# Sample states' old outputs in one padded tile, and side work of the projection in fewer groups

## The reference, cut to what matters

```python
inter = einsum('bthk,bhkv->bthv', qc * exp(b), state)         # outputs of the old states
att   = einsum('bthk,bshk,btshk->bhts', qc, kc, exp(diff))    # inside the chunk
new_state = state * exp(b_last)[..., None] + einsum('bshk,bshv->bhkv', kc * exp(b_last[:, None] - b), vc)
```

## Time and profile before

| what | value |
|---|---|
| median of the runs | 1394.96 us (1394.67 to 1395.44, 3 runs) |
| the profiled execution's own time | 1395.06 us |
| its span, first to last instruction | 1393.4 us |
| granted TensorE clock | 1.000 of full speed |
| PE busy | 1388.3 us (100% of the span) |
| DVE busy | 857.0 us (62%) |
| ACT busy | 583.3 us (42%) |
| POOL busy | 130.7 us (9%) |

### The profile page before, as it was taken

The page is one execution under the profiler, slowest core; times in us unless marked ns, Lnnn a source line. Parts: engine busy times, 40 slices in busy tenths (PEclk is TensorE's granted clock), DMA queues, the critical chain, the costliest instruction groups (busy, mean ns, idle before and its releaser), DMA issues.

```text
span 1393.4 us, 28677 instructions
## 1 busy us (share of the span) xinstructions
PE 1388.3 (100%) x10755; PEld 1375.1 (99%) x10755; DVE 857.0 (62%) x1178; ACT 583.3 (42%) x707; POOL 130.7 (9%) x214
## 2 busy tenths in 40 slices
PE   9999999999999999999999999999999999999999
PEld 9999999999999999999999999999999999999999
DVE  7778877657876555555554445555555556667554
ACT  7556744665334333333333333333333333335332
POOL 1523105001221000000000000000000001111000
PEclk9999999999999999999999999999999999999999
DMA  8756435446554545545445556545454545556553
GB/s 298 204 186 233 142 130 174 143 141 227 181 170 162 166 165 165 166 156 173 159 144 163 163 162 196 168 157 170 156 170 161 165 131 163 164 161 197 184 158 117
DMA packets 76905, 236.60 MB, mean 170 GB/s; under 512 B 14136, under 2 KB 14672, under 8 KB 76472
## 3 DMA queue, kind: packets, MB, share of 16 engines
q1 hardware_dynamic: 72072, 223.43, 50.2%
q0 software_dynamic: 3744, 11.22, 2.7%
q10 hardware_dynamic: 1040, 1.28, 0.3%
HBM read 231.34 MB, written 4.47 MB: 169 GB/s over the span
## 4 chain that ended last, share of the span: by engine, by line
PE 98%; ACT 1%; DVE 1%; DMA 0%; issue 0%; SPq 0%; DVEq 0%; ACTq 0%
PE acc L516 31%; PE acc L518 30%; PE acc L517 30%; PE px L1551 0%; PE px L1669 0%; PE px L1511 0%; PE px L1514 0%; PE px L1517 0%; DMA w_raw<-in_w_in 0%; PE px L1609 0%; PE px L516 0%; PE px L518 0%; PE px L517 0%; PE px L1736 0%; ACT w_hi L462 0%
## 5 line engine op out<-in xcount | busy, mean ns | idle before, releaser
L468 DVE TENSOR_TENSOR w_lo<-w_raw,w_hi 128x1024 fp32r<-128x1024 f32 (+3 forms) x446 | 509.8, 1148 | 313.9 <-ACT w_hi L462 305.0
L462 ACT ACTIVATE w_hi<-w_raw 128x1024 fp32r<-128x1024 f32 (+3 forms) x446 | 439.5, 988 | 551.2 <-PE acc L518 544.3
L516 PE MATMUL acc<-n_hi,w_hi 128*128 128x288 f32 x1664 | 492.5, 296 | 0.0
L517 PE MATMUL acc<-n_lo,w_hi 128*128 128x288 f32 x1664 | 490.9, 295 | 0.0
L518 PE MATMUL acc<-n_hi,w_lo 128*128 128x288 f32 x1664 | 489.2, 294 | 0.0
L518 PEld LDWEIGHTS acc<-n_hi,w_lo 128*128 128x128 f32 x1664 | 313.5, 188 | 0.0
L517 PEld LDWEIGHTS acc<-n_lo,w_hi 128*128 128x128 f32 x1664 | 312.4, 188 | 0.0
L516 PEld LDWEIGHTS acc<-n_hi,w_hi 128*128 128x128 f32 x1664 | 311.8, 187 | 0.0
L516 PE MATMUL acc<-x_hi,w_hi 128*128 128x288 f32 x816 | 244.9, 300 | 0.0
L517 PE MATMUL acc<-x_lo,w_hi 128*128 128x288 f32 x816 | 240.8, 295 | 0.0
L518 PE MATMUL acc<-x_hi,w_lo 128*128 128x288 f32 x816 | 240.0, 294 | 0.0
(11 more groups left out here) (304 smaller groups left out, 889.9 us busy)
## 6 DMA issues: line engine op xcount, KB each, us to landing
w_raw<-in_w_gu SPq DMA_DIRECT2D x176, 512.0 KB, 3.9
w_raw<-in_w_in SPq DMA_DIRECT2D x76, 512.0 KB, 4.3
w_raw<-in_w_down SPq DMA_DIRECT2D x64, 384.0 KB, 3.1
w_raw<-in_w_down SPq DMA_DIRECT2D x64, 320.0 KB, 3.1
w_raw<-in_w_ple SPq DMA_DIRECT2D x32, 576.0 KB, 3.7
w_raw<-in_w_out SPq DMA_DIRECT2D x32, 512.0 KB, 4.2
w_raw<-in_w_in SPq DMA_DIRECT2D x12, 256.0 KB, 6.2
proj<-in_xT SPq DMA_DIRECT2D x8, 288.0 KB, 6.6
```

The costliest lines, as they stand in the source:

```text
L462: nc.scalar.activation(whi[:, slot, 0:kt * P], raw[:, slot, 0:kt * P], ACT.Copy).then_inc(S("w_hi_done"), 1)
L468: nc.vector.tensor_tensor(wlo[:, slot, 0:kt * P], raw[:, slot, 0:kt * P], whi[:, slot, 0:kt * P].bitcast(F32), ALU.subtract).then_inc(S("w ...
L516: nc.tensor.matmul(out, w_h, row_of(m_hi_, k0 + k), start=first and k == 0, stop=False)
L517: nc.tensor.matmul(out, w_h, row_of(m_lo_, k0 + k), start=False, stop=False)
```

## The change

The kernel computes the same. The old states' outputs of all four heads now share one tile of 128 columns: `qes` places each head's queries at its own column, the 16 products add up in one place, the copy has 128 columns, and one product with a reordered identity brings them back, beside one product for the samples' inner part. The two first indexer groups are one visit (half 12), with the second in other banks. The levels are visited as (0,1), (2,3), (4,5), (6,7), (8), at halves 55, 57, 60, 63 and 67, the last together with `level_s`; the scaling for level 1 (`by_decays`) stays at 53. `kd_nat` moves to 69, its way back (`kd_back`) to 70, `state_p` to 73 behind `past`, both `state_s` to 80, `scan` to 38.

```diff
-    10: [("index", 0)],
-    12: [("index", 1)],
-    14: [("index", 2)],
-    18: [("index", 3), ("keys_i", 0)],
+    12: [("scores", (0, 1)), ("index", 0)],
+    13: [("index", 1)],
+    15: [("scores", (2,)), ("index", 2)],
+    18: [("scores", (3,)), ("index", 3), ("keys_i", 0)],
...
-    36: [("scan", 0), ("prior", 0)],
+    36: [("prior", 0)],
+    38: [("scan", 0)],
...
-    53: [("transpose_s", 1), ("level", 0)],
-    55: [("mix_s", 1), ("level", 1)],
+    53: [("transpose_s", 1), ("by_decays", 0)],
+    55: [("mix_s", 1), ("level", 0)],
     56: [("mix_s_back", 1)],
-    57: [("level", 2)],
+    57: [("level", 1)],
...
-    60: [("level", 3)],
-    63: [("level", 4)],
+    60: [("level", 2)],
+    63: [("level", 3)],
     64: [("last", 0)],
-    65: [("decayed", 0), ("level_s", 0)],
+    65: [("decayed", 0)],
     66: [("gelu_v", 0), ("norm_sq", 5)],
-    67: [("norm", 5), ("rooted", 5), ("scaled", 5), ("kd_nat", 0)],
-    68: [("norm_sq", 6), ("state_p", 0)],
-    69: [("norm", 6), ("rooted", 6), ("scaled", 6)],
-    70: [("pack", (ROW_VC, 1))],
+    67: [("norm", 5), ("level", 4), ("level_s", 0), ("rooted", 5), ("scaled", 5)],
+    68: [("norm_sq", 6)],
+    69: [("norm", 6), ("rooted", 6), ("scaled", 6), ("kd_nat", 0)],
+    70: [("pack", (ROW_VC, 1)), ("kd_back", 0)],
...
-    73: [("past", 0)],
+    73: [("past", 0), ("state_p", 0)],
...
-    77: [("out_norm", 0), ("state_s", 0)],
+    77: [("out_norm", 0)],
...
-    80: [("state_s", 1), ("gelu_u", 2)],
+    80: [("state_s", 0), ("state_s", 1), ("gelu_u", 2)],
...
-        VISITS = [(0,), (1, 2), (3, 4), (5, 6), (7, 8)]
+        VISITS = [(0, 1), (2, 3), (4, 5), (6, 7), (8,)]
+        SCALED = [(1, 2), (3, 4), (5, 6), (7,), ()]
...
-                A(past[:, :, :].rearrange("p a v -> p (a v)"), px[:, 4, :], ACT.Copy).then_inc(S("past_ready"), 1)
+                A(past, px[:, 4, 0:BDV], ACT.Copy).then_inc(S("past_ready"), 1)
...
-                for r in range(2):
-                    ins = A(ob[:, 2 * r:2 * r + 2, SEQ:T].rearrange("p e (b i) -> p e b i", b=NB),
-                            out_s(r).rearrange("p b e i -> p e b i"), ACT.Copy)
-                link(ins)
+                link(A(ob[:, :, SEQ:T], out_s.rearrange("p (q t) -> p q t", q=BH), ACT.Copy))
...
-                for m in (() if v == 4 else (2 * v, 2 * v + 1)):
+                for m in SCALED[v]:
+                    by_decays(m)
+            def by_decays(m):
+                dve.wait_ge(S("e_level"), m + 1)
...
-                    M(out_s(r), vbn_s, att_s[:, 2 * TS * r:2 * TS * r + 2 * TS].rearrange("p (e b i) -> p b e i", e=2, b=NB),
-                      start=r == 0, stop=False)
-                    for half in range(2):
-                        ins = M(out_s(r)[:, 4 * half:4 * half + 4, :, :], past[:, 2 * half + r, :],
-                                ident.rearrange("p (b n) -> p b n", b=4)[:, :, 0:2 * NS], start=False,
-                                stop=(r, half) == (1, 1))
-                ins.then_inc(S("o_mm"), 1)
+                M(out_s, vbn_s, att_s[:, :], start=True, stop=False)
+                M(out_s, past, ident.rearrange("p (b q i) -> p q b i", b=4, i=NS), start=False, stop=True).then_inc(S("o_mm"), 1)
...
-                        place = P * (2 * half + r)
                         for b in range(4):
-                            ins = M(px[32 * b:32 * b + 32, 4, place:place + P], qes[:, r, 4 * half + b, :],
-                                    s0[half][:, b, r, :], start=True, stop=True)
+                            ins = M(px[32 * b:32 * b + 32, 4, 0:BDV], qes[:, r, half, b, :], s0[half][:, b, r, :],
+                                    start=(half, r) == (0, 0), stop=(half, r) == (1, 1))
...
             def state_p(_):
                 pe.wait_ge(S("kdn_ready"), 1)
+                pe.wait_ge(S("gsum_ready"), 1)
```

More of the change, by code:

```diff
@@ L346, in build_layer @@
         qpad = soft[:, 2 * NR * SEQ:2 * NR * SEQ + NB * NG * 32].rearrange("p (b g n) -> p b g n", b=NB, g=NG)
-        past = vnat[:, :, :].rearrange("p a n -> p (a n)")[:, 0:4 * BDV].rearrange("p (a v) -> p a v", a=4)
+        past = vnat[:, :, :].rearrange("p a n -> p (a n)")[:, 0:BDV]
         vbn = soft[:, 0:3 * 512].rearrange("p (a n) -> p a n", a=3)
@@ L544, in build_layer, with index_bank @@
         levels = [P] + LEVELS
[L546 to L548 removed]
+        def index_bank(tt, q):
+            return (2 if q == 1 else 0) if tt else 4
         def level_bank(m):
[L552 removed]
+            return 4 if m % 2 else 0
         PARTS = {1: [(0, P, 0)], 2: [(0, 64, 64)], 3: [(0, 64, 0), (64, P, 64)]}
[L555 removed]
+        VISITS = [(0, 1), (2, 3), (4, 5), (6, 7), (8,)]
+        SCALED = [(1, 2), (3, 4), (5, 6), (7,), ()]
         def by_seq(ap):
@@ L1254, in level @@
                         dve.wait_ge(S("level_read"), m + 1)
-                for m in (() if v == 4 else (2 * v, 2 * v + 1)):
[L1256 to L1260, removed]
+                for m in SCALED[v]:
+                    by_decays(m)
+            def by_decays(m):
+                dve.wait_ge(S("e_level"), m + 1)
+                if m == 0:
+                    dve.wait_ge(S("lg_s"), 2)
+                    dve.wait_ge(S("qb_scaled"), 1)
+                    dve.wait_ge(S("acc_read"), kept(ROW_KB + 1))
+                e1, e2, _, _ = blocks(dd[:, m % 2, :, :], m)
+                q2, k1 = blocks(qb, m)[1], blocks(kb, m)[0]
+                V.tensor_tensor(blocks(qe[:, m % 2], m)[1], q2, e2, ALU.mult)
+                V.tensor_tensor(blocks(ke[:, m % 2], m)[0], k1, e1, ALU.mult).then_inc(S("level_ready"), 1)
             def level_s(_):
@@ L1285, in decayed @@
                 dve.wait_ge(S("e_last"), 1)
-                link(V.memset(qes[:, :, :, :], 0.0))
+                link(V.memset(qes[:, :, :, :, :], 0.0))
                 for e in range(2):
                     pp = slice(64 * e, 64 * e + 64)
-                    V.tensor_tensor(qes[pp, :, :, NS * e:NS * e + NS], by_seq(proj[pp, ROW_QB:ROW_QB + 2, SEQ:T]), by_seq(ebs[pp, :, :]),
-                                    ALU.mult)
+                    for half in range(2):
+                        for r in range(2):
+                            at, own = NS * (4 * r + 2 * e + half), slice(TS // 2 * half, TS // 2 * half + TS // 2)
+                            V.tensor_tensor(qes[pp, r, half, :, at:at + NS],
+                                            proj[pp, ROW_QB + r, SEQ:T][:, own].rearrange("p (b i) -> p b i", i=NS),
+                                            ebs[pp, r, own].rearrange("p (b i) -> p b i", i=NS), ALU.mult)
                 V.tensor_tensor(kdT[:, :, 0:SEQ], kb[:, :, 0:SEQ], dd[:, 1, :, 0:SEQ], ALU.mult)
@@ L1376, in _ @@
             stages = dict(weights=weights, index=index, index_end=index_end, values=values, transpose=transpose, pick=pick, pick_s=pick_s, norm_sq=norm_sq, scaled=scaled, prior=prior,
-                          softmax=softmax, exps=exps, gate=gate, scan=scan, level=level, level_s=level_s, last=last,
+                          softmax=softmax, exps=exps, gate=gate, scan=scan, level=level, by_decays=by_decays, level_s=level_s, last=last,
                           decayed=decayed, keys_s=keys_s, softmax_s=softmax_s, mix_s_back=mix_s_back, outputs=outputs,
@@ L1538, in weights, with scores @@
                 ins.then_inc(S("weights_mm"), 1)
-            def index(q):
-                pe.wait_ge(S("acc_read"), max(kept(ROW_QI + 2 * q + 1), kept(ROW_KI)))
+            def scores(quarters):
+                pe.wait_ge(S("acc_read"), max(kept(ROW_QI + 2 * quarters[-1] + 1), kept(ROW_KI)))
                 pe.wait_ge(S("ki_copied"), 16)
[L1544 to L1553, removed]
-                ins.then_inc(S("idx_mm"), 1)
+                if quarters[0]:
+                    pe.wait_ge(S("relu_done"), 2 * quarters[0])
+                else:
+                    pe.wait_ge(S("weights_done"), 1)
+                for q in quarters:
+                    for tt in range(2):
+                        nk, bank, at = P * (tt + 1), index_bank(tt, q), P if q == 1 and tt == 0 else 0
+                        for jj in range(2):
+                            for e in range(2):
+                                pp = slice(64 * e, 64 * e + 64)
+                                ins = M(px[:, bank + e, 256 * jj + at:256 * jj + at + nk],
+                                        proj[pp, ROW_QI + 2 * q + jj, P * tt:P * tt + P], proj[pp, ROW_KI if e else ROW_KD, 0:nk],
+                                        start=True, stop=True)
+                ins.then_inc(S("idx_mm"), len(quarters))
             def index_end(_):
```

39 lines of the change are left out of this document (19 added, 20 removed).

## The result

The changed kernel takes 1401.69 us in the median (1400.75 to 1402.03, 6 runs), the kernel before 1394.61 us beside it (1394.40 to 1395.44, 6 runs). The ratio is 1.0048, 95% interval 1.0039 to 1.0058: slower by 0.48%, some 7 us. The forecast was 1396.5 us, the range ended at 1398.6; both are missed. The profiled execution took 1400.75 us with a span of 1399.1, and is the fastest of the six. The other 1.4 us lie between executions of one program: the mean granted clock is 0.999 in the profiled execution and 0.997 to 0.998 in the five slower ones, so a longer stay at the lower clock may be part of them; they have no trace that would show it.

A forecast was written before the change was run, and what follows sets the result against it. PE, busy in the whole span, was taken to bound the kernel. Gains of -2.1 us up to half 77 and +3.7 us at the end gave +1.6 on 1395.06 us: 1396.5 us predicted, range 1392.8 to 1398.6.

The forecast's parts named there:

- The gains: On PE up to half 77: shorter visits and removed waits, -2.1 us in sum, between -1.4 and -2.7.
- the joined indexer groups: On PE: two indexer visits of the same form become one, two form changes fewer, -0.35 us.
- `state_p`: On PE, moved behind `past`: the wait ahead goes, -0.4 us, and one form change, -0.17, together -0.57 us.
- `outputs`: On PE: four records of 128 columns replace the short products and the step back to long ones, -0.8 us.
- the first transposes of probabilities: `scan` two halves later: DVE reaches the first softmax sooner and PE's wait goes, 0 to -0.2, taken as -0.2 us.
- the levels: On PE: visits of levels, `level_s` and `mix_s` go from 14 form changes to 13, -0.17 us.
- The 0.17 us for a change between unlike forms: On PE: changing 128 by 32 to 128 by 64 priced like the nearest row, full array to part, 0.17 us.
- DVE's addition: End of input projection, half 80: the added addition of `state_s` delays the last eviction, making PE 1.1 us later.
- the term of POOL's queue: Store ahead of `h`: queue 3.95 to 6.3 us later, taken as 5.1; `into_h` then makes PE 3.7 us late.
- C: First store holds POOL's queue in full ahead of `h`, waits add up in `into_h`: 1397.8 to 1399.3 us; chance 0.15.
- A: End of projection: only DVE is late, the last store lands before 339.7: sum -1.0, 1394.0 us; chance 0.17.
- B: End of projection costs nothing, DVE makes up the addition in gaps: 1392.5 us, or 1391.9; chance 0.13.

The follow-up runs named there:

- e1: Changed kernel with `state_s` 0 put back in half 77: 1392.96 us, ratio 0.9987 to the kernel before.
- e8: Kernel before with only the padded output tile (`qes`, `past`, `outputs` and their copies): 1393.73 us, ratio 0.9991 to the kernel before.
- e7: Changed kernel whose first store of states writes one of its four samples, 128 KB instead of 512: 1401.17 us, ratio 1.0046 to the kernel before.
- e11: Changed kernel with the hold of e9, and the load of `h` rows 4 to 15 waiting until the first store has landed: 1400.37 us, ratio 1.0034.
- e9: Changed kernel with SP holding the weight chunk of half 88 and all behind it until `h` rows 4 to 15 have landed: 1395.83 us, ratio 1.0005.
- e3: Changed kernel with the load of `h` rows 4 to 15 ahead of the first store on POOL: 1396.75 us, ratio 1.0016 to the kernel before.
- e5: Changed kernel with both the edit of e3 and that of e4: 1395.18 us, ratio 1.0002 to the kernel before.
- e6: Changed kernel with 34 unused products on PE ahead of the third tile of the output projection: 1399.78 us, ratio 1.0035 to the kernel before.
- e12: Changed kernel with the load of `h` rows 4 to 15 waiting until the first store has landed, no weight chunks held: 1402.33 us, ratio 1.0051.
- e2: Kernel before with only `state_s` 0 moved from half 77 to half 80: 1402.91 us, ratio 1.0058 to the kernel before.
- e4: Changed kernel with `into_h` waiting for the last store only at the second tile of each pair: 1396.88 us, ratio 1.0017 to the kernel before.
- e10: Changed kernel with the hold of e9 and the small first store of e7: 1395.16 us, ratio 1.0002 to the kernel before.

## Why the prediction was wrong

**The gains: the sum right, in part by luck.** Forecast -2.1, measured -2.06 us; e1 (-1.8) and e8 (-1.1 for its part) agree with the size. By visits: the joined indexer groups -0.38 (-0.35 forecast); `state_p`, with `past`, 2.28 against 1.69 + 1.20 = 2.89, so -0.61 (-0.57); `outputs` 3.13 against 4.02, -0.89 (-0.8); the first transposes of probabilities 0.97 against 1.39, -0.42 (-0.2). The visits of halves 53 to 69 together are 10.29 against 9.98 us, +0.31 where -0.17 was forecast. The wait ahead of norm 5 is 0.48 us of it, a term that the sum put at nothing and its bounds at 0.5; without it the levels come out at -0.17. The first transposes gained twice the forecast for the same reason turned round: the wait that the profile lists as 0.2 us had cost 0.4 from start to start. So two errors of one kind nearly cancelled. (The bounds of -1.4 and -2.7 are not added up in the prediction; its own small terms reach -1.2 at the low end.)

The 0.17 us for a change between unlike forms inside a visit, taken from the nearest row, held twice: `state_p` behind `past` saves 0.19 us beside its wait of 0.42, and the levels come out at -0.17. This agrees with the rule of the Trainium skill (TensorEngine Tiling (Array Packing), Key Properties) that was set beside it.

**DVE's addition: right.** +1.1 forecast, +1.14 measured, at the instruction named.

**The step that failed is the term of POOL's queue.** The forecast had PE 3.7 us late at the end, against half 77; it was 1.14 + 4.94 + 1.62 = 7.7 us. What was mis-sized is the transfer time of the load of `h` (7.3 us carried over, 11.1 measured) and, behind it, the price of a long wait of PE, where the slow clock was put at nothing. The 4.0 us between forecast and measurement are made up of three parts:

- *The landing, 2.4 us.* Against half 77, the last store landed at 342.92 + 2.06 = 344.98, and not at 342.55: 7.5 us later than before, beyond the bound of 6.3. That bound added up the later issue and the bytes of the store. The later issue was right (327.80 against the forecast 327.8). But the load of `h` then took 3.8 us longer. e7 shows that this isn't simply the bytes ahead of it, and e11 against e9, both without later chunks, that it is what is in flight when the load is issued (7.4 against 10.9 us). The next load on the queue follows 0.5 us behind in e11 and 4.6 in e9, but that doesn't explain it: in e3 it follows 11 us behind, and the load took 8.0. "Alone they took 2.9 us" and the 7.3 us of the load were durations on nearly idle engines; I carried the second over to a busy one. The 128 packets of the load show where the 3.8 us lie. Before, the first starts 1.2 us after the issue and the last 5.0 us behind the first; after, these are 2.9 and 6.8 us; the way from the last start to the landing adds 0.4. In e7 they are 1.4 and 8.6 us: the smaller store lets the first packet start earlier, and the spread gives it back. The spread comes of DMA engines that are out of step. In e9 50 packets start between 334 and 335 us and 88 in the next microsecond, and of these only 5 and 2 are the load's; the rest stand behind it in the queue, and so run on engines that have done their share. The landing waits for the last engine. Which engines lag, and why, stays open.
- *DVE's release, 0.3 us.* It began 0.32 us after the landing; 0.05 was allowed.
- *The clock, 1.6 us, less 0.3.* Nothing of it stood in the prediction. The 0.3 us come off because part of the lateness stood in another place than I said: the wait is ahead of the third tile, at half 86, where PE waits for accumulator 0 (`tile_free`) and had 339.81 - 338.98 = 0.83 us of slack, less the 0.14 us that PE takes from DVE's end to its start (343.69 to 343.83). My 0.35 us ahead of half 87 is real too (e5 and e6 wait there a second time), but with PE at 1.2 GHz DVE catches up first.

**The rivals.** C had the place and the sign right: the last store lands beyond the bound, and `into_h` waits for it. Its price was too low, 1397.8 at its bound and 1399.3 at its far end, which the range left out, and its mechanism, "the first store holds POOL's queue in full", is not what e7 shows: with a quarter of the store the load still took 10.9 us. I gave it 0.15 because I held the upper bound for one; it was built from durations of a less loaded stretch. A and B needed `into_h` released by PE, which of the changed kernel's versions only e1 shows beyond doubt.

**The shared queues, and the clock.** e9's shorter tail shows that weight chunks on SP's queue slow POOL's queue. How they share depends on when a chunk comes. In the kernel before, one issued 2.1 us behind the load (325.99) had no packet on the engines before 329.72, when the load was nearly through; from then on the queues took turns, 115 packets of POOL's and 117 of SP's between 331 and 334 us. In e12 the chunk issued 0.3 us behind the load shared with it one for one, and the load took 9.5 us instead of 7.4. The Trainium skill (DMA: Bandwidth & Descriptors, section Queues, rings and completion order) says that each engine takes queue rows in turn, packet by packet. The trace agrees for these stretches, and shows no turn in the 3.7 us that the first of these chunks waited. But I had used the rule for "share and not push, the landing stays at the lower end": the queues had shared in the kernel before too, so the rule gave no reason for the lower end, and sharing is itself a delay.

The granted clock was 0.50 after 4.8 us of waiting, and e6 made the span shorter by adding work. The Trainium skill (TensorE: Matmul & The Clock Gate, section Part 1: The HAM clock gate) says that the throttled state is the default and that activity releases it. The trace agrees, and the rule should have put a second term behind any PE wait of several us.

## What to carry to other kernels

Before a visit is moved, follow every DMA that its result releases, through its queue, to the instruction that waits for the last of them; here 0.35 us of saved mode changes cost 8 us (e2). A transfer's time read where the DMA engines were nearly idle was a lower bound elsewhere (7.3 against 9.5 to 11.6 us): before the move is priced, ask what will be in flight at its new start. Where a wait of PE reaches a few us, add the slow clock behind it, here 1.5 to 2.8 us. And read what a wait of PE costs from start to start: the listed idle time was short by 0.1 to 0.2 us.

## What the runs showed of the hardware that was not expected

- The granted clock fell to 0.50 in the profiled executions with waits of PE of 4.1 us and more (after, e2, e7, e11, e12), and with one of 2.3 us in that of e4; in those with waits of 1.5 us and less (e3, e5, e6, e9, e10) it stayed at 1.00 behind the wait. The time lost to it differed: 1.6 us in the changed kernel and e7, 1.5 in e4, 1.9 in e2, 2.5 in e11 and 2.8 in e12, each as the sum of the steps over 0.133 us behind the wait. In e11 one of the five executions has a mean clock of 1.000 and is 1.9 us faster than the next. In e4 the mean clock parts the executions cleanly (0.999 for the four slowest); in e3 the three slowest (1398.00 to 1398.73) have 0.999, but so has the fastest, so there this mean doesn't decide it.
- A load of 1.7 MB took 7.3 to 8.0 us when issued on idle or nearly idle DMA engines and 9.5 to 11.6 among other transfers, and shrinking the store ahead of it from 512 to 128 KB moved that by 0.2 us (after, e7).
- Holding three weight chunks back, on another queue, until the load had landed brought the loss against the kernel before from 7.1 us to 0.8 (after, e9).
